# A mixture-of-experts kernel: the expert slot table from products of one-hot matrices instead of scattered stores

## What is computed

```python
def moe(h, prm):
    t = h.reshape(B * N, D)
    scores = jax.nn.sigmoid((t @ prm["w_router"]).astype(jnp.float32))
    _, idx = lax.top_k(scores + prm["b_router"].astype(jnp.float32), TOP_K)      # 4 of 32 experts
    sel = jnp.take_along_axis(scores, idx, axis=-1)
    w = sel / jnp.sum(sel, axis=-1, keepdims=True) * ROUTED_SCALE
    comb = jnp.sum(jax.nn.one_hot(idx, N_EXPERTS, dtype=jnp.float32) * w[..., None], axis=1)
    gate = jnp.einsum("td,edf->tef", t, prm["w_gate_e"])
    up = jnp.einsum("td,edf->tef", t, prm["w_up_e"])
    act = jax.nn.silu(gate) * up * comb[..., None].astype(t.dtype)
    routed = jnp.einsum("tef,efd->td", act, prm["w_down_e"])
    shared = (jax.nn.silu(t @ prm["w_gate_s"]) * (t @ prm["w_up_s"])) @ prm["w_down_s"]
    return (routed + shared).reshape(B, N, D)
```

## Time and profile before

| | us |
|---|---|
| median of three runs | 1747.09 |
| the three runs | 1743.97 to 1747.53 |
| the profiled execution | 1745.84 |
| its span, from the first to the last instruction | 1744.0 |
| TensorE busy in the span | 1571.9 (90%) |
| VectorE, ScalarE, GpSimd busy | 738.6, 457.3, 290.3 |

### The profile page before, as it was taken

The page is one execution under the profiler, slowest core; times in us unless marked ns, Lnnn a source line. Parts: engine busy times, 40 slices in busy tenths (PEclk is TensorE's granted clock), DMA queues, the critical chain, the costliest instruction groups (busy, mean ns, idle before and its releaser), DMA issues. The chain is left out here.

```text
span 1744.0 us, 21593 instructions
## 1 busy us (share of the span) xinstructions
PE 1571.9 (90%) x7262; PEld 1017.9 (58%) x7262; DVE 738.6 (42%) x1405; ACT 457.3 (26%) x906; POOL 290.3 (17%) x526
## 2 busy tenths in 40 slices
PE   5999999999988898999999996999999869778886
PEld 3677566677766644444444443776799545444442
DVE  1577778778876321111111126345655611111112
ACT  2322234333324410111111104333554501111111
POOL 3000000001112042222222220000001034333320
PEclk7999999999999998999999998999999989899898
DMA  9742340355584325888898856302154649999993
GB/s 328 242 169 100 121 146 1 111 181 194 173 309 148 141 105 201 317 317 322 318 336 322 327 178 232 125 28 97 49 215 173 253 176 401 414 414 415 416 386 140
DMA packets 123989, 394.11 MB, mean 226 GB/s; under 512 B 16468, under 2 KB 21028, under 8 KB 104464
## 3 DMA queue, kind: packets, MB, share of 16 engines
q1 hardware_dynamic: 104128, 359.42, 55.2%
q0 software_dynamic: 18432, 30.56, 5.1%
q10 hardware_dynamic: 1360, 3.23, 0.5%
HBM read 389.88 MB, written 30.61 MB: 241 GB/s over the span
## 5 line engine op out<-in xcount | busy, mean ns | idle before, releaser
L1493 PE MATMUL ps<-ring,oT_b 128*128 128x512 f32 x512 | 226.5, 595 | 0.0
L1499 PE MATMUL ps<-ring,oT_b 128*64 128x256 f32 x1152 | 155.8, 431 | 45.4 <-DMA ring<-in_w_up_e 45.4
L2026 DVE TENSOR_TENSOR head<-ps,head 128x128 f32<-128x128 f32 (+1 forms) x68 | 24.1, 355 | 404.7 <-ACT head L1109 389.8
L1493 PEld LDWEIGHTS ps<-ring,oT_b 128*128 128x128 f32 x512 | 95.5, 192 | 108.1 <-issue 108.1
L1499 PEld LDWEIGHTS ps<-ring,oT_b 128*64 128x64 f32 x1152 | 93.6, 156 | 99.2 <-DMA ring<-in_w_up_e 39.2
L1379 PE MATMUL ps<-ring_lo,w_hi 128*128 128x512 f32 (+1 forms) x384 | 132.3, 344 | 3.9 <-DVE ring_lo L1851 3.7
L1664 DVE SCALAR_TENSOR_TENSOR Grow<-ring,small,Grow 128x512 f32<-128x512 f32 x182 | 131.2, 749 | 3.8
L1380 PE MATMUL ps<-h_lo,w_hi 128*128 128x512 f32 (+1 forms) x384 | 130.5, 340 | 0.0
L1109 ACT ACTIVATE head<-ps 128x128 f32<-128x128 f32 (+1 forms) x68 | 22.3, 328 | 400.5 <-PE ps L1493 209.3
L785 POOL TENSOR_TENSOR qkv<-qkv,head 128x512 f32<-128x512 f32 (+1 forms) x32 | 36.1, 1127 | 431.3 <-DVE head L1883 431.3
L1278 PE MATMUL ps<-ring_lo,oT_lo 128*128 128x512 f32 (+1 forms) x256 | 87.2, 341 | 5.1 <-DVE ring_lo L1708 4.7
(11 more groups left out here) (305 smaller groups left out, 2970.4 us busy)
## 6 DMA issues: line engine op xcount, KB each, us to landing
ring<-in_w_gate_e SPq DMA_DIRECT2D x68, 1024.0 KB, 7.8
ring<-in_w_up_e SPq DMA_DIRECT2D x68, 1024.0 KB, 10.8
ring<-in_w_ada SPq DMA_DIRECT2D x34, 1024.0 KB, 5.3
qkv<-in_w_down_e SPq DMA_DIRECT2D x34, 1024.0 KB, 5.3
ring<-in_w_in SPq DMA_DIRECT2D x13, 2048.0 KB, 10.2
cT<-in_w_down_e SPq DMA_DIRECT2D x17, 1024.0 KB, 5.3
fT<-in_w_down_e SPq DMA_DIRECT2D x17, 1024.0 KB, 5.3
qkv<-in_w_in SPq DMA_DIRECT2D x7, 2048.0 KB, 10.5
```

What stands on the lines that cost most here:

```text
L1493: ins = nc.tensor.matmul(ps[:, o:o + 512], x[:, tile(k)], gu[u][:, :, k, :], start=k == 0, stop=k == KC - 1)
L1499: ins = nc.tensor.matmul(ps[64 * f:64 * f + 64, o:o + 256], xk, w, start=k == 0, stop=k == KC - 1, skip_group_check=True)
```

## The change

The table is made on the chip. A choice with rank r and expert e belongs in row r mod `CAP` and column 32 x (r div `CAP`) + e. Two kinds of one-hot matrices say this, with the 128 tokens of a tile along the partitions: `row_of_item` has for each choice a 1 in the choice's column, and `id_of_item` has the id + 1 in the choice's row. TensorE sums the products of the two over all tiles and choices in one PSUM bank (the new group `table`), 16 products of 128x128 in layer 0 and 8 in layer 1; both factors are stored as rounded fp32, which TensorE takes in one record. Where the sum is 0 the place is empty. The numbers 0 to 127 along the columns, and the same mod `CAP`, come from one more product of the matrices in `tri` (the new group `columns`), for which VectorE has four instructions ahead of `needed`.

The DRAM table, its clearing, the indirect stores, the read-back and their waits are gone from GpSimd. On VectorE `place` and the conversion `posu` go; the picking by one-hot stays and now reads the ranks from PSUM; then come five operations on the 16 (8) ranks, one operation that makes all `row_of_item`, 16 (8) that make an `id_of_item` each, and after the product three that make `row_y` from the sum. The operations for `row_g` now come before those for `turn`, not after `items`. ScalarE's first silu, which waited for the positions, waits for the first `id_of_item`.

```diff
+        g.add("dve", l, "columns")
         g.add("dve", l, "rank")
         g.add("act", l, "sgu", 0, 0)
+        g.add("dve", l, "table")
...
+        column_of, rank_of = qkv[:, 256:256 + P], qkv[:, 384:384 + P]
+        id_of = qkv[:, 688:704].rearrange("p (t k) -> p t k", k=TOPK)
+        row_of_item = m_lo[:, 4:8, :].rearrange("p a b -> p (a b)").rearrange("p (n c) -> p n c", c=P)
+        id_of_item = oT_lo[:, :, :].rearrange("p a b -> p (a b)").rearrange("p (n c) -> p n c", c=P)
+        absent = qkv[:, 512:512 + P]
...
-                pool.dma_start(slots_d[l], C["absent"][0:P * act * NE]).then_inc(table_clear, 16)
-                pool.wait_ge(table_clear, 16 * (l + 1))
-                pool.wait_ge(pos_ready, l + 1)
-                for t in range(act):
-                    for k in range(TOPK):
-                        pool.indirect_dma_start(out=slots_d[l], out_offset=bass.IndirectOffsetOnAxis(ap=posu[:, t, k:k + 1], axis=0),
-                                                in_=pick_id[:, t, k:k + 1], in_offset=None,
-                                                bounds_check=P * act * NE - 1, oob_is_err=False).then_inc(table_filled[l], 16)
-                pool.wait_ge(table_filled[l], 16 * act * TOPK)
-                for p0 in range(0, P, CAP[l]):
-                    pool.dma_start(row_y[p0:p0 + CAP[l], 0:P], slots_d[l].rearrange("(r j e) a -> j r (e a)", e=NE, j=CAP[l]))\
-                        .then_inc(table_read[l], 16)
-                pool.dma_start(row_y[:, P:P + 1], C["absent"][0:P]).then_inc(table_read[l], 16)
...
-                act_e.wait_ge(pos_ready, l + 1)
+                act_e.wait_ge(id_ready, NTILE * TOPK * l + 1)
...
+                ones, above = tri[:, 0:P], tri[:, P:2 * P]
+                dst = group(l, "columns")
+                pe.wait_ge(tri_loaded, 16 * (l + 1))
+                nc.tensor.matmul(dst[:, 0:P], ones, above, start=True, stop=True).then_inc(psum_full, 1)
...
+                dst = group(l, "table")
+                for n in range(act * TOPK):
+                    pe.wait_ge(id_ready, NTILE * TOPK * l + n + 1)
+                    ins = nc.tensor.matmul(dst[:, 0:P], id_of_item[:, n, :], row_of_item[:, n, :], start=n == 0, stop=n == act * TOPK - 1)
+                ins.then_inc(psum_full, 1)
...
+                wait_full(dve, l, "columns")
+                V.tensor_scalar(id_of[:, 0:act], pick_id[:, 0:act], 1.0, None, ALU.add)
+                V.tensor_copy(column_of, bank(l, "columns")[:, 0:P])
+                link(V.tensor_scalar(rank_of, bank(l, "columns")[:, 0:P], float(CAP[l]), -float(CAP[l]), ALU.is_ge, ALU.mult))
+                V.tensor_tensor(rank_of, rank_of, bank(l, "columns")[:, 0:P], ALU.add).then_inc(emptied["dve"], 1)
+                wait_emptied(dve, l, "columns")
                 wait_full(dve, l, "rank")
                 ranks = bank(l, "rank")
                 V.tensor_tensor(needed, ranks[:, P:P + 1], item_t[:, l:l + 1], ALU.is_gt).then_inc(needed_ready, 1)
-                V.scalar_tensor_tensor(place[:, 0:act], ranks[:, 0:NE * act].rearrange("p (t e) -> p t e", e=NE), float(NE),
-                                       iota[:, 0:NE].rearrange("p (a e) -> p a e", a=1).to_broadcast([P, act, NE]),
-                                       ALU.mult, ALU.add).then_inc(emptied["dve"], 1)
+                pick(pos[:, 0:act], ranks[:, 0:NE * act].rearrange("p (t e) -> p t e", e=NE))
+                rank, turns_of = pos[:, 0:act], turn_of[:, 0:act]
+                dve.wait_ge(grow_stored, 48)
+                link(V.tensor_scalar(turns_of, rank, float(CAP[l]), None, ALU.is_ge))
+                for r in range(2, ROUNDS):
+                    link(V.scalar_tensor_tensor(turns_of, rank, float(CAP[l] * r), turns_of, ALU.is_ge, ALU.add))
+                V.scalar_tensor_tensor(rank, turns_of, -float(CAP[l]), rank, ALU.mult, ALU.add)
+                link(V.scalar_tensor_tensor(turns_of, turns_of, float(NE), idxf[:, 0:act, 0:TOPK], ALU.mult, ALU.add))
+                n_id = act * TOPK
+                columns = turns_of.rearrange("p t (k a) -> p (t k) a", a=1)
+                V.tensor_tensor(row_of_item[:, 0:n_id, :], column_of.rearrange("p (a c) -> p a c", a=1).to_broadcast([P, n_id, P]),
+                                columns.to_broadcast([P, n_id, P]), ALU.is_equal).then_inc(emptied["dve"], 1)
                 wait_emptied(dve, l, "rank")
-                pick(pos[:, 0:act], place)
-                dve.wait_ge(grow_stored, 48)
-                V.tensor_copy(posu[:, 0:act], pos[:, 0:act]).then_inc(pos_ready, 1)
+                for n in range(n_id):
+                    t, k = divmod(n, TOPK)
+                    V.tensor_scalar(id_of_item[:, n, :], rank_of, pos[:, t, k:k + 1], id_of[:, t, k:k + 1],
+                                    ALU.is_equal, ALU.mult).then_inc(id_ready, 1)
+                wait_full(dve, l, "table")
+                ids = bank(l, "table")[:, 0:P]
+                V.tensor_scalar(row_y[:, P:P + 1], iota[:, 0:1], 0.0, float(ABSENT), ALU.mult, ALU.add)
+                link(V.tensor_scalar(absent, ids, 0.5, float(ABSENT + 1), ALU.is_lt, ALU.mult))
+                V.scalar_tensor_tensor(row_y[:, 0:P], ids, -1.0, absent, ALU.add, ALU.add).then_inc(emptied["dve"], 1)
+                wait_emptied(dve, l, "table")
+                split = P // CAP[l]
+                ins = V.tensor_scalar(row_g[l], row_y, 2, None, ALU.logical_shift_right)
+                if split == 2:
+                    link(ins)
+                    link(V.tensor_scalar(row_g[l], row_g[l], 2.0, half_id, ALU.mult, ALU.add))
+                    ins = V.tensor_scalar(row_y, row_y, 2.0, half_id, ALU.mult, ALU.add)
+                ins.then_inc(rows_ready, 1)
...
-                def make_rows():
-                    split = P // CAP[l]
-                    dve.wait_ge(table_read[l], 16 * split + 16)
-                    ins = V.tensor_scalar(row_g[l], row_y, 2, None, ALU.logical_shift_right)
-                    if split == 2:
-                        link(ins)
-                        link(V.tensor_scalar(row_g[l], row_g[l], 2.0, half_id, ALU.mult, ALU.add))
-                        ins = V.tensor_scalar(row_y, row_y, 2.0, half_id, ALU.mult, ALU.add)
-                    ins.then_inc(rows_ready, 1)
-                make_rows()
```

More of the change, by code:

```diff
@@ L320, in hybrid_layers @@
         tri = qkv[:, 0:256]
+        column_of, rank_of = qkv[:, 256:256 + P], qkv[:, 384:384 + P]
[3 more added lines that the diff above has]
+        absent = qkv[:, 512:512 + P]
         oh_tmp = tmp2[:, 0, :].rearrange("p (t k e) -> p t k e", t=NTILE, k=TOPK)
-        turn = qkv[:, 384:384 + MAX_ITEMS]
-        place = qkv[:, 256:384].rearrange("p (t e) -> p t e", e=NE)
+        turn = qkv[:, 640:640 + MAX_ITEMS]
         score_T = tmp2[0:NE, 1, :]
@@ L398, in hybrid_layers @@
         tri_loaded = one("tri_loaded")
-        table_clear = one("table_clear")
-        pos_ready = one("pos_ready")
+        id_ready = one("id_ready")
         needed_ready = one("needed_ready")
         turn_ready = one("turn_ready")
-        table_filled = by_layer("table_filled")
-        table_read = by_layer("table_read")
         rows_ready = one("rows_ready")
```

5 lines of the change are left out of this document (1 added, 4 removed).

## The result

| | before | after |
|---|---|---|
| median of four runs each, side by side | 1746.18 us | 1729.98 us |
| lowest and highest | 1743.97 to 1747.53 | 1728.68 to 1732.51 |
| the profiled execution, its span | 1745.84, 1744.0 | 1732.51, 1730.7 |

The ratio is 0.991, with a 95% interval of 0.9893 to 0.9927: 16.2 us faster. The forecast was 1728.5 us in a range of 1723 to 1737.

What follows compares the result with a forecast made beforehand. Ahead of the expert loops, the table's read-back and first gather were taken to bound the start. Gains of 7.1 us (layer 0) and 12.8 (layer 1) made 19.9, less 2.6 for one clock loss: 17.3, so 1728.5 us, range 1723 to 1737.

Steps and rivals of the forecast that it cites:

- Layer 0's start, 2.9 us: Ahead of layer 0's expert loop: TensorE takes the first token rows at 658.2 instead of 661.12, 2.9 us earlier.
- Transposes and first product, 2.7 and 1.5: Layer 0: transposes and copy 2.75 us for 5.5, saving 2.7; first gate and up product 7.0 for 8.51, saving 1.5.
- Layer 1's start, 9.1: Ahead of layer 1's loop: TensorE takes the first rows at 1414.1 instead of 1423.21, 9.1 us earlier.
- Transposes and copy: Layer 1, ahead of the first gate and up product: 2.8 us down to 1.5, saving 1.3 us.
- First product of layer 1, 2.4: Layer 1's first gate and up product: 5.99 us down to 3.6 at full clock, saving 2.4 us.
- The clock, one of three places, 2.6 us: Before both loops and around layer 1's table: half clock may cost up to 2.6 us each; one lost, chance 0.42.
- VectorE's chain in layer 0, 0.8 us to spare: Layer 0: VectorE's one-hots end at 632.3, hidden behind TensorE's first shared product ending at 633.15, 0.8 us to spare.
- weights bind layer 1 anyway: Rival, layer 1's loop: its earlier start is lost, 1738.7 us; chance 0.08 together with a late gather.
- Slower by the id products: Rival, both tables: VectorE's id products pace them far slower than 0.2 us each, 1749.7 us at 1.225; chance 0.03.
- Late gather: Rival, both layers: first gather stays last, half the gain gone, some 1736 us; chance 0.08 together with layer 1 bound.
- the first shared product of layer 0 escapes its loss by `columns` alone: Layer 0, within the clock-kept rival (none lost, 0.27): `columns` fills the gap, sparing 2.6 us, 1723.3 us.
- VectorE's fixed price: VectorE's id products: each instruction pays a fixed price; 0.13 us estimated by the skill page, 0.2 us kept from the row.

Runs made afterwards that it cites:

- after_again: The changed kernel, same program, measured and profiled once more: 1728.68 us, ratio 0.9895 against the kernel before.
- id_forms: The changed kernel with 40 more VectorE instructions in layer 0, rows of eight with different operand forms, behind `items`: 1728.21 us in one run.
- warm: The changed kernel with TensorE multiplying unread data in its two short waits ahead of each layer's loop: 1731.7 us, ratio 0.9911 against the kernel before.
- ids_twice: The changed kernel with VectorE making eight id products per layer twice, the extra ones into spare memory: 1734.51 us, ratio 0.994 against the kernel before.
- only_l1: The changed kernel in layer 1 only, the kernel before with its DRAM table in layer 0: 1737.02 us, ratio 0.9945 against the kernel before.
- gather_delayed: The changed kernel with 24 small GpSimd multiplications behind its wait for `items`, ahead of its gathers: ratio 0.9942 against the kernel before.

## Why the prediction held, step by step

- **Layer 0's start, 2.9 us**: 2.90 in the profile (the transposes start 661.12 - 619.75 = 41.37 us behind the ranks' start before, 38.47 after). Right, with its parts: shared end at +2.04 (1.80 from the ranks' start), wait 1.76 us, ended by no gather.
- **Transposes and first product, 2.7 and 1.5**: 2.62 and 1.48 in after_again, and 1.8 and -0.7 in after, where the clock was lost. The three terms together are 7.05 in the one and 4.0 in the other. The mechanism and the sum of 7.1 hold; how much of it is seen depends on the clock. (Two groups of 8 at 0.12 and a copy of 0.7 make 2.6, not the 2.75 of the sum; 2.87 was measured.)
- **Layer 1's start, 9.1**: 8.7 (first transposes 29.32 behind the ranks' start before, 20.64 after; shared end 3.4 later and not 3.0). The mis-sized term is the id product: 0.26 us each (4.18 for 16) for 0.2, which is 0.5 for eight. I took it from a row with one column operand, and id_forms shows the second to cost the difference. Transposes and copy gave 0.9 for 1.3: they take 1.82 us, not 1.5.
- **First product of layer 1, 2.4**: 0.7 in after (6.03 to 5.36 us, clock partly lost), 2.4 in after_again, where the second shared product lost 1.7 instead. C came to 10.3 for 12.8; with 1.7 for the clock back it would be 12.0, and id_forms, where none is lost, has 11.9.
- **The clock, one of three places, 2.6 us**: after had two lost of the places I named, after_again one. Their sizes were 3.0 us in layer 0 and 1.7 in layer 1, for the 2.6 forecast. What I had not seen is that the mixing part, which the edit doesn't touch, loses 2.3 to 3 us in some executions and not in others, and that D differs by some 2 us; either can hide what is won at a named place (warm: both first products at full clock, no time gained). With the clock kept the two layers would give 7.05 + 12.0 = 19.05 us, 0.85 under the sum of 19.9; the medians gave 16.2. The 2.9 us between are near the 2.6 forecast, but they are what a subtraction leaves, and hold the chance differences of B and D as well. The profiled executions of this routing lost two, one and none of the three places (after, after_again, id_forms), so that the median came within 1.5 us of "one lost" is in part luck.
- **VectorE's chain in layer 0, 0.8 us to spare**: it ended at 632.98 for 632.3, and TensorE's first shared product at 633.41, so 0.4. The one-hot of columns took 2.29 for 2.45. The table's products took 2.30 us for 1.95, inside the bounds. But the end of the shared product isn't the limit: ids_twice put 2.1 us into the chain and 0.36 came through, so the room is some 1.7 us, because each product needs only its own id.
- **The rivals**: weights bind layer 1 anyway: no, D is 294.77 for 294.98 (296.98 in after_again, which takes back 2 of 10.3), and only_l1 is 9.4 us faster. Slower by the id products: it wanted 1.06 us each, and they are 0.26. Late gather: not in after; gather_delayed shows that in layer 1 it lies one load of weights away. That the first shared product of layer 0 escapes its loss by `columns` alone: no, 9.75 us; two wider products are what it took.
- **VectorE's fixed price**: the Trainium skill (VectorE: DVE Perf Modes, section on the TRN2 errata) gives 58 cycles and the number of elements divided by the factor of the mode; without a faster mode that is an estimate of 0.194 us here, and the row with one column operand agrees at 0.20 from start to start. My estimate of 0.13 took two elements a cycle, which no row shows for these operands. And the two rows that I compared, 128 and 1024 elements, are of different operations (a tensor with a column, and two tensors), so they don't show a fixed price by themselves.

## What to carry to other kernels

A DRAM table that is scattered and read back costs the latency that the trace shows between the last store and the first reader (1406.7 to 1417.94 in layer 1); a product of two one-hots puts it on an engine that stands idle then, but count what this puts ahead of it in that engine's queue. Sum such an edit only up to the next thing that is late: here a 13.33 us wait was worth 10 to 12. And give TensorE's clock a term of its own at each place where the engine pauses or is left with small products: a fifth to a third of this gain was to be had by filling the old waits. Before you read a gain out of one profile, take a second one of the same program, and compare stretches that the edit doesn't touch: here they differ by up to 3 us.

## What the runs showed of the hardware

- Two executions of one program lose the clock in different places: in layer 1 the first gate and up product in after (5.36 us for 3.67), the second shared one in after_again (5.39 for 3.70), none in id_forms. Stretches that no edit touched differed by it, too (B 377.0 to 380.0). Only the loss behind the ranks of layer 0 came in every profile without fillers ahead of them.
- Small products that follow another engine one by one take its pace: eight table products took 2.04 us behind VectorE's 0.26 us each, and 1.19 with all ids ready.
- Layer 1's first gather, an indirect one of 128 rows, landed in 3.19 us while the transfers' share was 0.20 (before, 1419.97 to 1423.2), and in 6.59 us behind 2 MB of weights, at a share of 0.89 (gather_delayed).
- A second operand with one value for each partition adds 0.06 us to a 0.20 us VectorE instruction on 128x128 elements; rounding the output adds nothing to speak of.

What stays open: what decides in an execution which of these places gets the slow clock, and why D was 2.2 us longer in after_again than in after. Ahead of the ninth expert of layer 1 TensorE waits 2.96 us for weights in after_again and 0.80 in after; no run isolates that.
